# Mixer B's decode attention on the matrix engine, its K and V on GpSimd's queue

## The chip, the cores and the metric

One core of a Trainium2 chip runs one launch of the kernel. The metric is the device time of a launch in microseconds (us). The engines are PE (TensorE), DVE (VectorE), ACT (ScalarE) and POOL (GpSimd); SP issues most transfers. Each engine works through its own list of instructions in order and waits on semaphores for the others.

## What is computed

One layer of a hybrid decoder, at once for a prompt of 256 positions and for 8 decode samples of one position each (position 2048), 264 tokens in all:

- `h = RMSNorm(x)`, `z = h @ w_in`, cut into q, k, v of mixer A (16 heads, 2 kv heads) and of mixer B (16 heads of 64), with partial rotary on q and k.
- Mixer A: window of 128, with a learned sink for each head.
- Mixer B: keys at distances 0, d, 2d, ..., w for (w, d) = (128, 1), (512, 4), (2048, 16), merged by the branches' softmax denominators. For a decode sample these are 320 different keys of the cache and the sample's own, 321 in all; a key in several branches counts as often. With one softmax over the 321 keys, and log(count) added to the score, numerator and denominator are those of the merge:

```python
s = einsum('nqhd,nqjhd->nqhj', q, k[:, idx]) * 64 ** -0.5
p = exp(s - max(s)); l = sum(p); num = einsum('nqhj,nqjhd->nqhd', p, v[:, idx])
o_b = sum(exp(m - m_star) * num) / sum(exp(m - m_star) * l)      # over the three branches
```

- `x += RMSNorm(concat(RMSNorm(oA), RMSNorm(oB)) @ w_out)`, then a gated feed-forward part with a causal convolution of width 3.

## The kernel before

**Weights.** Everything is held transposed: 128 features on the partitions, 264 tokens along the row. Weights come in 364 chunks of 512 KB through a ring of four slots. For each chunk SP loads `raw`, ACT rounds it to `wh` (L499), DVE takes the rest as `wl` (L722), and PE does 24 matmuls, 8 tiles by 3 products: wh x hi, wh x lo, wl x hi (L1171 to L1173). SP loads chunk n once DVE has split chunk n-4; at step n ACT splits chunk n+3 and DVE chunk n+2, and then each does the stages of step n.

**The plan.** The first 84 steps (68 chunks of `w_in`, 16 of `w_out`) carry the attention between the chunks. `STEP` gives a step for each stage, `make_plan` writes `PLAN[n]`, and every engine goes through the same `PLAN[n]` after its part of chunk n. The three column groups of pair t (t = 0 to 3: four heads of mixer B, q, k and v) end at steps 12t+4, 12t+8 and e = 12t+12; they are taken out of PSUM by `evac` on DVE, which rotates q and k (L731 to L734). The prompt's heads follow as S (scores, L1234 and L1235), T (transposes of the probabilities, L1243) and V (values, L1260 to L1262), four heads in each pair.

**Mixer B, decode.** A unit u = 2t+v is two heads of all 8 samples; there are eight. Its stages before:

- `qk` (step e-3): PE transposes q and k of the 8 samples (L1209), ACT copies them (L529) and stores q to DRAM.
- `qI`: SP adds the samples' own key to `Kd` and loads q back, the same for all 128 partitions (`qb`, L434).
- `mul`: POOL multiplies `Kd`, keys on the partitions and 3 x 8 x 128 along the row, by `qb` (L1069). `bS`: DVE sums over the 64 features of each head (L872).
- `bT`: PE transposes the scores to 16 rows of 321 (L1297); DVE adds the mask and takes the minimum (L879), ACT does the exponentials (L571), DVE scales by 1/sum (L884).
- `pO`, `pI`: ACT stores the probabilities, SP loads them back spread over 2 x 64 partitions (`Pb`, L444).
- `bM`: POOL copies the own value in (L1076) and multiplies `Pb` by `Vd` (L1078). `bV`: ACT sums over the keys, 8 instructions (L582).

`Kd`, `Vd`, `qb`, `Pb` have one buffer each. SP loads K and V of the next unit (L450, L451, L457) in its own line with the weights, six steps ahead of the stage, after waiting for the reader of the buffer.

**Shared PSUM bank.** Of eight banks four take the projections, three the prompt's heads, and one, `B_M`, all the rest, in the order of the list `MISC`. PE waits in `take_misc` until the stage before has been copied out:

```python
n = misc(kind, *a)
if n:
    pe.wait_ge(misc_free, n)
```

V of the prompt is transposed in `vtr` (L1219) and copied by ACT (L518). Behind mixer B follow its norms (`N`, `W`, `ND`, from step 59 on), mixer A's heads (steps 57 to 74) and mixer A's decode attention, which is done by matmuls: `aload` (K and V, L1082, on POOL's queue, after the last sum of mixer B), `aS` (16 matmuls, L1269) and `aV` (16 matmuls, L1289).

Of the kernel before, what the change touches and what calls it, by code (L numbers as in the profile page):

```python
# [27 lines left out]
P = 128  # L28
# [8 lines left out]
NEG = 1e30  # L37
# [13 lines left out]
AHEAD = 6  # L51
# [46 lines left out]
def group_end(gi):  # L98
# [34 lines left out]
def make_plan():  # L133
# [8 lines left out]
    for t in range(4):  # L142
# [3 lines left out]
        add(e + STEP["qk"][0], "qk", t)  # L146
        add(e + 1, "vtr", t)
        for a in range(4):
            s0 = e + STEP["s"][t] + gap * a
            add(s0, "S", t, a)  # L150
            add(s0 + STEP["T"][t], "T", t, a)
            add(s0 + STEP["V"][t], "V", t, a)
        add(s0 + STEP["V"][t], "O", t)
        for v in range(2):
            add(e + STEP["qI"][v], "qI", 2 * t + v)
            add(e + STEP["mul"][v], "mul", 2 * t + v)
            add(e + STEP["bS"][v], "bS", 2 * t + v)
            add(e + STEP["bT"][v], "bT", 2 * t + v)
            add(e + STEP["pO"][v], "pO", 2 * t + v)
            add(e + STEP["pI"][v], "pI", 2 * t + v)  # L160
            add(e + STEP["bM"][v], "bM", 2 * t + v)
# [29 lines left out]
for _n in sorted(PLAN):  # L191
    for _s in PLAN[_n]:
# [3 lines left out]
        if s[0] in ("ss", "qk", "vtr", "vdec", "aS", "aT", "aR", "aV", "W", "ND", "bT")]  # L196
# [45 lines left out]
def build(nc, d, q_dram, p_dram):  # L242

    ctx = ExitStack()
    with ctx:
# [26 lines left out]
        with ExitStack() as att:  # L272
# [10 lines left out]
            qk = sa("qk", [NDEC, 512])  # L283
            vself = sa("vself", [P, 4, 2, NDEC])
# [13 lines left out]
            bSc = sa("bSc", [P, 48])  # L298
            bSm = sa("bSm", [16, KB])
            bP = sa("bP", [16, KB])  # L300
# [33 lines left out]
        bmn, bl, bri = (small[0:16, c:c + 1] for c in (78, 79, 80))  # L334
# [31 lines left out]
        Kd_landed, Kd_full, Vd_landed = sem("Kd_landed"), sem("Kd_full"), sem("Vd_landed")  # L366
        q_out, qb_landed, p_out, Pb_landed = sem("q_out"), sem("qb_landed"), sem("p_out"), sem("Pb_landed")
        kq_ready = sem("kq_ready")
        bS_ready, bV_ready = sem("bS_ready"), sem("bV_ready")
        vp_ready = sem("vp_ready")  # L370
# [7 lines left out]
        zero_ready = sem("zero_ready")  # L378
# [29 lines left out]
        def _(sp):  # L408
# [7 lines left out]
            def stage(kind, *a):  # L416
                if kind == "ss":

                    sp.wait_ge(misc_ready, misc("ss") + 1)
                    sp.wait_ge(zero_ready, 1)  # L420
                    load_K(0)
                    load_V(0)
                elif kind == "bS" and a[0] + 1 < OT:
                    load_K(a[0] + 1)
                elif kind == "bM" and a[0] + 1 < OT:
                    load_V(a[0] + 1)
                elif kind == "qI":

                    u, = a
                    t, v = u // 2, u % 2  # L430
                    sp.wait_ge(misc_free, misc("qk", t) + 1)
                    sp.dma_start(Kd[64:65, 2], qk[:, 256 + P * v:256 + P * v + P]).then_inc(Kd_full, 16)
                    sp.wait_ge(q_out, 16 * (t + 1))
                    sp.dma_start(qb[:], q_dram[t, :, P * v:P * v + P].unsqueeze(0).to_broadcast([P, NDEC, P])  # L434
                                 ).then_inc(qb_landed, 16)
                elif kind == "pI":

                    u, = a
                    sp.wait_ge(p_out, 16 * (u + 1))
                    if u:  # L440
                        sp.wait_ge(bV_ready, u)
# [1076 lines left out]
```

## Time and profile before

| what | value |
|---|---|
| three runs | 1321.42, 1323.63, 1326.42 us |
| median | 1323.63 us |
| span of the profiled execution | 1329.0 us |
| time around that span | none is given; the span is 5.4 us above the median |
| PE, DVE, ACT, POOL busy | 91, 60, 43, 17% of the span |
| mean granted PE clock | 0.951 of full speed (2.4 GHz) |
| moved by DMA | 236.99 MB |

The profile is of one execution. Times in its rows are us from the first instruction. Busy time of an engine is the union of its instructions' durations. PE's matmuls overlap each other in the records, so the pace of PE is read from start to start, not from durations. An fp32 matmul leaves two records, each with its weight load; one of fp32r, and a transpose, leave one. PEclk is the share of full speed that was granted: 1.00 is 2.4 GHz, 0.50 is 1.2 GHz, and a value between is a mean over a stretch that had both.

### The profile page before, as it was taken

What the parts mean: (1) busy time and instruction counts of PE and PEld (TensorE: products, weight loads), DVE (VectorE), ACT (ScalarE), POOL (GpSimd) and SP (SyncE); (2) the same over time, 40 slices, a digit from 0 to 9 for tenths busy, and PEclk for the clock granted to TensorE, in tenths of its full rate; (3) what the DMA queues carried; (4) which work ended last, traced back from release to release, by engine and by line L of the source; (5) the groups of instructions that cost most, each with busy time, mean ns of one, the idle gap of its engine ahead of it and who ended that gap; (6) DMA issues with size and microseconds to landing.
All of it is one profiled execution on the core that took longest, in us unless ns stands there. A gap on an engine that the chain in (4) does not pass through costs nothing.

```text
span 1329.0 us, 24539 instructions
## 1 busy us (share of the span) xinstructions
PE 1210.8 (91%) x9379; PEld 1182.2 (89%) x9379; DVE 791.0 (60%) x987; ACT 571.7 (43%) x938; POOL 223.3 (17%) x148
## 2 busy tenths in 40 slices
PE   5987687797989895999999999999999999999994
PEld 5987676786779895999999999999999999999994
DVE  5666969675644558665556655556655644454445
ACT  4334343446544364544444444444444433343331
POOL 2053525260200023410100100001010000020003
PEclk9998898897978997999999999999999999999997
DMA  6676969695522451455555555555555666656641
GB/s 250 230 236 219 294 196 282 202 260 147 140 80 80 140 166 58 146 188 173 189 187 174 173 167 189 184 189 167 169 185 174 205 187 176 183 178 179 184 143 65
DMA packets 83163, 236.99 MB, mean 178 GB/s; under 512 B 7432, under 2 KB 32368, under 8 KB 82032
## 3 DMA queue, kind: packets, MB, share of 16 engines
q1 hardware_dynamic: 81728, 232.30, 56.1%
q0 software_dynamic: 1072, 3.90, 0.9%
q8 instruction: 29, 0.48, 0.2%
q10 hardware_dynamic: 320, 0.20, 0.1%
q14 instruction: 14, 0.11, 0.0%
HBM read 231.13 MB, written 5.20 MB: 178 GB/s over the span
## 4 chain that ended last, share of the span: by engine, by line
PE 77%; DVE 10%; issue 5%; DMA 3%; ACT 2%; POOL 1%; SPq 0%; ACTq 0%; DVEq 0%; POOLq 0%
PE ps L1171 24%; PE ps L1172 24%; PE ps L1173 24%; DVE wl L722 2%; DMA raw<-in_w_in 2%; DVE bSc L872 1%; DVE bP L884 1%; PE ps L1235 1%; PE ps L1234 1%; DVE hl L957 1%; DVE xT L967 1%; DMA qb<-q_dram 1%; POOL Kd L1069 1%; PE ps L1243 1%; PE ps L1200 1%
## 5 line engine op out<-in xcount | busy, mean ns | idle before, releaser
L1171 PE MATMUL ps<-hh,wh 128*128 128x264 f32 x2080 | 610.2, 293 | 33.8 <-DVE wl L722 23.4
L1173 PE MATMUL ps<-hh,wl 128*128 128x264 f32 x2080 | 602.0, 289 | 0.0
L722 DVE TENSOR_TENSOR wl<-raw,wh 128x1024 fp32r<-128x1024 f32 x364 | 465.0, 1295 | 199.4 <-ACT wh L499 199.3
L1172 PE MATMUL ps<-hl,wh 128*128 128x264 f32 x1952 | 566.9, 290 | 0.0
L499 ACT CAST wh<-raw 128x1024 fp32r<-128x1024 f32 x364 | 374.9, 1045 | 352.1 <-PE ps L1173 276.6
L1171 PEld LDWEIGHTS ps<-hh,wh 128*128 128x128 f32 x2080 | 404.0, 194 | 44.8 <-DVE wl L722 27.2
L1173 PEld LDWEIGHTS ps<-hh,wl 128*128 128x128 f32 x2080 | 402.1, 193 | 0.0
L1172 PEld LDWEIGHTS ps<-hl,wh 128*128 128x128 f32 x1952 | 378.6, 194 | 0.1
L1172 PE MATMUL ps<-gl,wh 128*128 (+1 forms) x704 | 200.7, 285 | 0.0
L1171 PE MATMUL ps<-gh,wh 128*128 (+1 forms) x704 | 200.1, 284 | 0.0
L1173 PE MATMUL ps<-gh,wl 128*128 (+1 forms) x704 | 199.8, 284 | 0.0
L1172 PEld LDWEIGHTS ps<-gl,wh 128*128 128x128 f32 x704 | 132.7, 188 | 0.0
L1173 PEld LDWEIGHTS ps<-gh,wl 128*128 128x128 f32 x704 | 132.6, 188 | 0.0
L1171 PEld LDWEIGHTS ps<-gh,wh 128*128 128x128 f32 x704 | 132.5, 188 | 0.0
L1136 POOL COPY co<-U 128x4 f32 (+1 forms) x22 | 21.2, 963 | 395.7 <-DVE U L984 395.7
L1069 POOL TENSOR_TENSOR Kd<-Kd,qb 128x3072 f32<-128x3072 f32 x8 | 55.1, 6892 | 62.1 <-DMA qb<-q_dram 62.1
L983 DVE TENSOR_TENSOR U<-ps,rB 128x512 f32<-128x512 f32 x22 | 15.2, 692 | 75.2 <-PE ps L1173 75.1
L1078 POOL TENSOR_TENSOR Pb<-Pb,Vd 128x2568 f32<-128x2568 f32 x8 | 45.7, 5707 | 76.6 <-DMA Pb<-p_dram 76.6
L1003 DVE TENSOR_TENSOR up<-ps,rB 128x528 f32<-128x528 f32 x22 | 15.6, 707 | 69.5 <-PE ps L1173 69.5
L677 ACT ACTIVATE cv<-U,par 128x280 f32<-128x280 f32 x44 | 25.0, 616 | 64.3 <-DVE U L984 64.3
L1152 POOL TENSOR_TENSOR up<-up,ysq 128x528 f32<-128x528 f32 x5 | 9.6, 1918 | 243.2 <-ACT ysq L709 242.7
L991 DVE SCALAR_TENSOR_TENSOR cv<-U,par,cv 128x280 f32<-128x280 f32 x88 | 41.0, 507 | 11.4 <-ACT cv L677 8.3
(213 smaller groups left out, 1087.6 us busy)
## 6 DMA issues: line engine op xcount, KB each, us to landing
raw<-in_w_gate SPq DMA_DIRECT2D x88, 512.0 KB, 4.0
raw<-in_w_up SPq DMA_DIRECT2D x88, 512.0 KB, 4.6
raw<-in_w_down SPq DMA_DIRECT2D x88, 512.0 KB, 3.6
raw<-in_w_in SPq DMA_DIRECT2D x68, 512.0 KB, 6.6
raw<-in_w_out SPq DMA_DIRECT2D x32, 512.0 KB, 3.8
Pb<-p_dram SPq DMA_DIRECT2D x16, 642.0 KB, 8.8
Vd<-in_vb SPq DMA_DIRECT2D x8, 1280.0 KB, 8.4
Kd<-in_kb SPq DMA_DIRECT2D x8, 1024.0 KB, 5.7
```

The lines of the kernel that those rows point to most:

```text
L499: nc.scalar.copy(wh[:, slot], raw[:, slot]).then_inc(hi_ready, 1)
L677: nc.scalar.activation(cv[:, k], U[:, k, 0:NU - 2], ACT.Identity, scale=par[:, bass.ds(i * 2 + (C_CW + k), 1)], bias=par[:, bass.ds(i * 2 ...
L722: V.tensor_tensor(wl[:, slot], raw[:, slot], wh[:, slot].bitcast(F32), ALU.subtract).then_inc(lo_ready, 1)
L983: line.do(V.tensor_tensor(U[:, :, 2:2 + SEQ], ps[:, 0:2, 0:SEQ], wide(rB[:, 0:SEQ]), ALU.mult))
L991: ins = V.scalar_tensor_tensor(cv[:, k], U[:, k, tap:tap + NU - 2], par[:, bass.ds(i * 2 + (C_CW + FT * tap + k), 1)], cv[:, k], ALU.mult, ...
L1003: V.tensor_tensor(up[:], ps[:, 2:4, 0:TOK], wide(rB[:]), ALU.mult).then_inc(up_taken, 1)
L1069: G.tensor_tensor(Kd[:], Kd[:], qb[:].unsqueeze(1).to_broadcast([P, 3, NDEC, P]), ALU.mult).then_inc(kq_ready, 1)
L1078: G.tensor_tensor(Pb[:], Pb[:], Vd[:], ALU.mult).then_inc(vp_ready, 1)
L1136: line.do(G.tensor_copy(co[:, bass.ds(i * 2, 2), 0:2], U[:, :, SEQ:SEQ + 2]))
L1171: nc.tensor.matmul(out, a, x, start=start, stop=False)
L1172: nc.tensor.matmul(out, a, xl, start=False, stop=False)
L1173: return nc.tensor.matmul(out, b, x, start=False, stop=stop)
```

## The change

Mixer B's decode scores and values are computed by matmuls, with K held features-first and V keys-first (the arrays `kb` and `vb` swap their layouts on the host).

- Gone: `qk`, `qI`, `mul`, `bT`, `pO`, `pI`, `bM`, the two DRAM buffers, the buffers `Kd`, `qb`, `Vd`, `Pb`, and all of SP's stages (SP now loads only weights here). DVE's copy `vself` and its memset of `Kd` go too.
- `qsel` (POOL, step e-3, both units): the own key is copied into `Kt`, then q of the samples into `Qsel`, a zeroed array with 32 columns for each sample of which two are filled (one head each).
- `bS` (PE, steps e-2 and e+3): eight fp32 matmuls, 32 weight columns by 321 moving ones; sample 4q+j goes to PSUM partitions 32j to 32j+31, and q = 0 and 1 add up there. DVE's mask and ACT's exponential follow as before, on 128 partitions in place of 16. POOL then loads K for two units later; `Kt` has two buffers.
- `bR` (e, e+5): PE transposes the probabilities (three), ACT copies them to `pT`.
- `bV` (e+3, e+8): 24 fp32 matmuls, three blocks of keys for each of 8 samples, 128x128 weights from `Vk`, two moving columns; ACT copies out the two heads. POOL then loads V of the next unit into the one buffer `Vk`.
- `vdx` (e+1, right behind `vtr`): PE transposes v of the samples (two), ACT copies them to `v8`, POOL's queue brings them into row 64 of `Vk`'s last block.

```diff
@@ -104,17 +103,13 @@
-    "qI": [-3, 2],
-    "mul": [-2, 4],
-    "bS": [2, 6],
-    "bT": [3, 11],
-    "pO": [3, 11],
-    "pI": [3, 12],
-    "bM": [7, 15],
-    "bV": [8, 16],
+    "qsel": [-3, -3],
+    "vdx": [1],
+    "bS": [-2, 3],
+    "bR": [0, 5],
+    "bV": [3, 8],
-    "qk": [-3],
...
@@ -152,13 +147,9 @@
-            add(e + STEP["qI"][v], "qI", 2 * t + v)
-            add(e + STEP["mul"][v], "mul", 2 * t + v)
+            add(e + STEP["qsel"][v], "qsel", 2 * t + v)
-            add(e + STEP["bT"][v], "bT", 2 * t + v)
-            add(e + STEP["pO"][v], "pO", 2 * t + v)
-            add(e + STEP["pI"][v], "pI", 2 * t + v)
-            add(e + STEP["bM"][v], "bM", 2 * t + v)
+            add(e + STEP["bR"][v], "bR", 2 * t + v)
...
@@ -193,7 +184,7 @@
         ORDER.setdefault(_s[0], []).append(_s[1:])
 MISC = [s for n in sorted(PLAN) for s in PLAN[n]
-        if s[0] in ("ss", "qk", "vtr", "vdec", "aS", "aT", "aR", "aV", "W", "ND", "bT")]
+        if s[0] in ("ss", "vtr", "vdx", "vdec", "aS", "aT", "aR", "aV", "W", "ND", "bS", "bR", "bV")]
 def number(kind, *args):
...
@@ -307,10 +298,8 @@
-                Kd = sb("Kd", [P, 3, NDEC, P], F32, a2)
-                qb = sb("qb", [P, NDEC, P], F32, a2)
-                Vd = sb("Vd", [P, NDEC, KB], F32, a2)
-                Pb = sb("Pb", [P, NDEC, KB], F32, a2)
+                Kt = sb("Kt", [P, 2, NDEC, KB], F32, a2)
+                Vk = sb("Vk", [P, 3, NDEC, P], F32, a2)
...
@@ -519,17 +460,12 @@
+                elif kind == "vdx":
+                        act.wait_ge(Vk_full, 16 * 2 * t)
+                    nc.scalar.copy(v8[:], ps[0:NDEC, B_M, 0:256]).then_inc(misc_free, 1)
...
@@ -565,24 +501,26 @@
+                elif kind == "bS":
+                    if u:
+                        act.wait_ge(misc_ready, misc("bR", u - 1) + 1)
+                elif kind == "bR":
+                    act.wait_ge(misc_ready, misc(kind, *a) + 1)
+                    line.do(nc.scalar.copy(pT[:, 0:256], ps[:, B_M, 0:256]))
+                    nc.scalar.copy(pT[0:65, 256:384], ps[0:65, B_M, 256:384]).then_inc(misc_free, 1)
+                elif kind == "bV":
+                    act.wait_ge(misc_ready, misc(kind, *a) + 1)
+                    for h in range(2):
+                        ins = nc.scalar.copy(od[64 * h:64 * h + 64, 0, u], ps[64 * h:64 * h + 64, B_M, h:h + 15:2])
+                        if h == 0:
+                    ins.then_inc(misc_free, 1)
...
@@ -864,20 +799,12 @@
-                    u, = a
-                    dve.wait_ge(kq_ready, u + 1)
-                    if u:
-                        dve.wait_ge(misc_ready, misc("bT", u - 1) + 1)
-                    V.tensor_reduce(bSc[:], Kd[:].rearrange("p c s (h e) -> p (c s h) e", h=2), AX.X,
-                                    ALU.add).then_inc(bS_ready, 1)
-                elif kind == "bT":
-                        dve.wait_ge(p_out, 16 * u)
+                        dve.wait_ge(b_exp, u)
-                        out=bSm[:], in0=ps[0:16, B_M, 0:KB], in1=tab[0:16, T_MD:T_MD + KB], scale=1.0, scalar=NEG,
+                        out=bSm[:], in0=ps[:, B_M, 0:KB], in1=tab[:, T_MD:T_MD + KB], scale=1.0, scalar=NEG,
...
@@ -1060,25 +987,50 @@
+                elif kind == "ss":
+                    pool.wait_ge(misc_ready, misc(kind) + 1)
+                    load_K(0)
+                    load_V(0)
+                    load_K(1)
+                elif kind == "qsel":
+                    t, v = u // 2, u % 2
+                    pool.wait_ge(Kt_landed[v], 16 * (t + 1))
+                    pool.wait_ge(evac_done, GI[("kB", t)] + 1)
+                    if u:
+                        pool.wait_ge(qsel_ready, 3 * u)
+                    G.tensor_copy(Kt[:, v, :, KEYS_B], ks[:, t % 2, v, SEQ:TOK]).then_inc(qsel_ready, 1)
+                    place = Qsel[:, v].rearrange("p (q r) -> p q r", q=2)
+                    q2 = qs[:, t % 2, v, SEQ:TOK].rearrange("p (q j) -> p q j", q=2)
+                    for h in range(2):
+                        pool.wait_ge(qsel_ready, 3 * u + 1 + h)
+                        G.tensor_copy(place[64 * h:64 * h + 64, :, h:h + 97:32],
+                                      q2[64 * h:64 * h + 64]).then_inc(qsel_ready, 1)
+                elif kind == "bS":
+                    if u + 2 < OT:
+                        pool.wait_ge(misc_ready, misc(kind, *a) + 1)
+                        load_K(u + 2)
+                elif kind == "vdx":
+                    t, = a
+                    pool.wait_ge(misc_free, misc(kind, *a) + 1)
+                    load_vself(2 * t)
+                elif kind == "bV":
+                    u, = a
+                    if u + 1 < OT:
+                        pool.wait_ge(misc_ready, misc(kind, *a) + 1)
+                        load_V(u + 1)
+                        if u % 2 == 0:
+                            load_vself(u + 1)
+                    pool.wait_ge(misc_ready, misc("bV", OT - 1) + 1)
...
@@ -1088,6 +1040,18 @@
+            def load_K(u):
+                G.dma_start(Kt[:, u % 2], d["kb"][u]).then_inc(Kt_landed[u % 2], 16)
+            def load_V(u):
+                G.dma_start(Vk[:, 0:2], d["vb"][u, :, 0:2]).then_inc(Vk_landed, 16)
+                G.dma_start(Vk[0:64, 2], d["vb"][u, 0:64, 2]).then_inc(Vk_landed, 16)
+            def load_vself(u):
+                v = u % 2
+                G.dma_start(Vk[64:65, 2], v8[:, P * v:P * v + P]).then_inc(Vk_full, 16)
+            G.memset(Qsel[:], 0.0)
...
@@ -1199,15 +1163,12 @@
+                elif kind == "vdx":
+                    pe.wait_ge(evac_done, GI[("vB", t)] + 1)
+                    for m in range(2):
+                        ins = nc.tensor.transpose(ps[0:NDEC, B_M, P * m:P * m + P], vT[:, m, SEQ:TOK], ident[:])
...
@@ -1290,12 +1251,34 @@
-                elif kind == "bT":
-                    pe.wait_ge(bS_ready, a[0] + 1)
+                elif kind == "bS":
+                    u, = a
+                    pe.wait_ge(qsel_ready, 3 * (u + 1))
+                    take_misc(kind, *a)
+                    v = u % 2
+                    for q in range(2):
+                        for j in range(4):
+                            ins = nc.tensor.matmul(ps[32 * j:32 * j + 32, B_M, 0:KB],
+                                                   Qsel[:, v, P * q + 32 * j:P * q + 32 * j + 32],
+                                                   Kt[:, v, 4 * q + j], start=q == 0, stop=q == 1)
+                    ins.then_inc(misc_ready, 1)
+                elif kind == "bR":
+                    u, = a
+                    pe.wait_ge(b_p, u + 1)
-                        ins = nc.tensor.transpose(ps[0:16, B_M, k0:k1], bSc[0:k1 - k0, 16 * c:16 * c + 16],
-                                                  ident[0:k1 - k0, 0:k1 - k0])
+                        ins = nc.tensor.transpose(ps[0:k1 - k0, B_M, P * c:P * c + P], bP[:, k0:k1], ident[:])
+                    ins.then_inc(misc_ready, 1)
+                elif kind == "bV":
+                    u, = a
+                    pe.wait_ge(Vk_landed, 32 * (u + 1))
+                    pe.wait_ge(Vk_full, 16 * (u + 1))
+                    take_misc(kind, *a)
+                    for s in range(NDEC):
+                        r = 32 * (s % 4) + 2 * (s // 4)
+                        for c, (k0, k1) in enumerate(KSPLIT_B):
+                            ins = nc.tensor.matmul(ps[:, B_M, 2 * s:2 * s + 2], Vk[0:k1 - k0, c, s],
+                                                   pT[0:k1 - k0, P * c + r:P * c + r + 2], start=c == 0, stop=c == 2)
```

## Rows read from the trace of the kernel before

**Rows 1.** The page: the span, and PE's busy time.

```profile
span 1329.0 us, 24539 instructions
PE 1210.8 (91%) x9379; PEld 1182.2 (89%) x9379; DVE 791.0 (60%) x987; ACT 571.7 (43%) x938; POOL 223.3 (17%) x148
```

**Rows 2.** Windows: busy us (x instructions) by engine, PEclk, DMA share, GB/s; then L722's own.

```profile
47.80:316.10 268.30, 216.10 (x1541) 202.06 (x1540) 200.49 (x237) 115.10 (x282) 105.53 (x33) 0.90 0.79 239
590.00:690.00 100.00, 100.00 (x819) 100.00 (x818) 60.25 (x76) 44.08 (x56) 10.05 (x15) 1.00 0.56 177
...
47.80:316.10 268.30, 87.09 (x53) 0.90 0.79 239
316.10:459.00 142.90, 29.20 (x24) 0.87 0.36 102
590.00:690.00 100.00, 39.74 (x34) 1.00 0.56 177
```

**Rows 3.** Groups by line and shape, 0 to 520 us: busy us, mean ns, idle before.

```profile
L722 DVE TENSOR_TENSOR wl<-raw,wh 128x1024 fp32r<-128x1024 f32 x102 | 146.4, 1444 | 37.8 <-ACT wh L499 37.7
L1069 POOL TENSOR_TENSOR Kd<-Kd,qb 128x3072 f32<-128x3072 f32 x8 | 55.1, 6892 | 62.1 <-DMA qb<-q_dram 62.1
L884 DVE TENSOR_SCALAR bP<-bP,small 16x321 f32<-16x321 f32 x8 | 29.5, 3691 | 0.3
L582 ACT ACTIVATE Pb<-Pb 128x321 f32<-128x321 f32 x64 | 29.1, 457 | 1.8 <-POOL Pb L1078 1.8
L872 DVE TENSOR_REDUCE bSc<-Kd 128x48 f32<-128x3072 f32 x8 | 26.8, 3344 | 6.7 <-POOL Kd L1069 6.7
L518 ACT COPY vn<-ps 128x512 f32<-128x512 f32 x4 | 2.3, 586 | 3.9 <-PE ps L1219 3.9
```

**Rows 4.** Timeline of POOL, then of DVE, 138 to 155 us: start us, us, instruction.

```profile
138.74 5.69 POOL L1078 TENSOR_TENSOR Pb<-Pb,Vd 128x2568 f32<-128x2568 f32 x1 [9.59 <-DMA Pb<-p_dram]
147.34 6.99 POOL L1069 TENSOR_TENSOR Kd<-Kd,qb 128x3072 f32<-128x3072 f32 x1 [2.91 <-DMA qb<-q_dram]
...
139.45 5.16 DVE L884 TENSOR_SCALAR bP<-bP,small 16x321 f32<-16x321 f32 x1
147.81 7.08 DVE L734 TENSOR_TENSOR qs<-r,sh 128x528 f32<-128x528 f32 x1
```

**Rows 5.** Timeline of PE, 69 to 71 us and 76 to 78 us.

```profile
69.14 0.60 PE L1219 MATMUL ps<-ident,vT 128*128 128x128 f32 x4
69.67 0.49 PE L1234 MATMUL ps<-ks,qs 64*128 64x128 f32 x2
69.99 0.59 PE L1235 MATMUL ps<-ks,qs 64*128 64x256 f32 x2
70.52 0.39 PE L1171 MATMUL ps<-hh,wh 128*128 128x264 f32 x1
...
76.78 0.33 PE L1260 MATMUL ps<-vn,PT 128*128 128x64 f32 x2
77.47 0.45 PE L1297 MATMUL ps<-ident,bSc 128*16 128x128 f32 x3
```

**Rows 6.** Windows around mixer A's decode matmuls, columns as in rows 2.

```profile
392.60:394.30 1.70, 1.70 (x27) 1.62 (x27) 1.54 (x5) 0.74 (x3) 0.00 (x0) 0.99 0.07 22
394.30:401.10 6.80, 6.80 (x37) 6.76 (x35) 1.39 (x5) 1.61 (x5) 0.00 (x0) 0.50 0.27 77
418.60:421.50 2.90, 2.90 (x21) 2.66 (x19) 0.00 (x0) 2.48 (x6) 0.00 (x0) 1.00 0.00 1
421.50:425.30 3.80, 3.80 (x16) 3.53 (x15) 0.00 (x0) 3.41 (x8) 0.00 (x0) 0.51 0.00 0
425.30:428.40 3.10, 3.10 (x15) 3.10 (x15) 2.86 (x8) 0.00 (x0) 0.00 (x0) 0.50 0.00 0
```

**Rows 7.** Waits of SP's queue, 47.8 to 316.1 us; POOL's timeline at 354 us.

```profile
SPq L450 <- DVE bSc L872: 33.3, 7, 8.2
...
354.01 0.59 POOL L1082 DMA_DIRECT2D KtA<-in_ka  x1 [12.16 <-ACT Pb L582]
```

More of the change, by code:

```diff
@@ L145, in make_plan @@
         gap = STEP["gap"][t]
-        add(e + STEP["qk"][0], "qk", t)
         add(e + 1, "vtr", t)
+        add(e + STEP["vdx"][0], "vdx", t)
         for a in range(4):
@@ L297, in build @@
             rd = sa("rd", [P, 3, NDEC])
[L298 to L300 removed]
+            bSm = sa("bSm", [P, KB])
+            bP = sa("bP", [P, KB])
             with ExitStack() as a2:
@@ L333, in build @@
         amn, al, aes, ari = (small[:, c:c + 1] for c in (74, 75, 76, 77))
-        bmn, bl, bri = (small[0:16, c:c + 1] for c in (78, 79, 80))
+        bmn, bl, bri = (small[:, c:c + 1] for c in (78, 79, 80))
         sinkn = small[:, 82:82 + H_A + 1]
@@ L365, in build @@
         KtA_landed, VtA_landed, VtA_full = sem("KtA_landed"), sem("VtA_landed"), sem("VtA_full")
[L366 to L370, printed above, removed]
+        Kt_landed = [sem(f"Kt_landed{c}") for c in range(2)]
+        Vk_landed, Vk_full = sem("Vk_landed"), sem("Vk_full")
+        qsel_ready = sem("qsel_ready")
         norm_a = sem("norm_a")
@@ L414, in load @@
                 sp.dma_start(raw[:, slot], src).then_inc(raw_landed[slot], 16)
[L416 to L427, printed above, removed]
-                    u, = a
[L430 to L439, printed above, removed]
-                    if u:
-                        sp.wait_ge(bV_ready, u)
-                    for h in range(2):
-                        src = p_dram[u].rearrange("(s h) k -> h s k", h=2)[h].unsqueeze(0)
-                        sp.dma_start(Pb[64 * h:64 * h + 64], src.to_broadcast([64, NDEC, KB])).then_inc(Pb_landed, 16)
-            def load_K(u):
-                if u:
-                    sp.wait_ge(bS_ready, u)
-                sp.dma_start(Kd[:, 0:2], d["kb"][u, :, 0:2]).then_inc(Kd_landed, 16)
-                sp.dma_start(Kd[0:64, 2], d["kb"][u, 0:64, 2]).then_inc(Kd_landed, 16)
-            def load_V(u):
-                if u:
-                    sp.wait_ge(vp_ready, u)
-                sp.dma_start(Vd[:, :, 0:KEYS_B], d["vb"][u]).then_inc(Vd_landed, 16)
             sp.dma_start(par[:, 0:C_CW], d["par"][:, 0:C_CW]).then_inc(gains_landed, 16)
@@ L469, in _ @@
                 load(chunk(n, 0, 4, 0), d["w_in"][GROUPS[n // 4][2], n % 4])
-                for s in PLAN.get(n - AHEAD, ()):
-                    stage(*s)
             with sp.Fori(0, (N_OUTA + N_OUTB) // 4) as i:
@@ L747, in evac @@
                     dve.wait_ge(v_stored, 16 * 4)
-                    dve.wait_ge(misc_ready, misc("vtr", 3) + 1)
+                    dve.wait_ge(misc_ready, misc("vdx", 3) + 1)
                     line.do(V.tensor_tensor(vT[:, 0], src[:, 1], rB[:], ALU.mult))
@@ L780, in evac @@
                         dve.wait_ge(v_stored, 16 * t)
-                        dve.wait_ge(misc_ready, misc("vtr", t - 1) + 1)
-                    line.step(V.tensor_tensor(vT[:], src, wide(rB[:]), ALU.mult))
-                    V.tensor_copy(vself[:, t], vT[:, :, SEQ:TOK]).then_inc(evac_done, 1)
+                        dve.wait_ge(misc_ready, misc("vdx", t - 1) + 1)
+                    V.tensor_tensor(vT[:], src, wide(rB[:]), ALU.mult).then_inc(evac_done, 1)
             def stage(kind, *a):
@@ L798, in stage @@
                     line.step(V.memset(qA[:], 0.0))
-                    V.memset(Kd[64:128, 2], 0.0).then_inc(zero_ready, 1)
                 elif kind == "S":
```

63 lines of the change are left out of this document (12 added, 51 removed).

## The prediction

> **What bounds the kernel now.** I read the page first: PE is busy 1210.8 of 1329.0 us [rows 1], so the question is where the rest of PE's time is and whether mixer B's decode work owns it. The splits of L722, one for each weight chunk, give the pace: 34 in 100 us from 590 to 690, so 2.94 us a chunk when nothing but weights is multiplied, with PE at 100 of 100 us and a granted clock of 1.00 [rows 2]. The change touches nothing after the projections, so that stage stays as it is. From 47.8 to 316.1, where mixer B's prompt and decode attention run, 53 splits take 268.3 us, PE is busy 216.1 and the clock is 0.90 [rows 2].
>
> I take those 268.3 us apart. Chunks: 53 x 2.94 = 155.8. A prompt head costs PE 0.85 for its scores (69.67 to 70.52), about 0.40 for three transposes and 0.69 for its values (76.78 to 77.47) [rows 5]; 16 heads x 1.94 = 31.0. The transposes of V take 0.53 (69.14 to 69.67) [rows 5], four times 2.1; the transposes "qk" are as many and as large, 2.0; those of the scores ("bT") three each time, 0.40 x 8 = 3.2. That makes 194 us of work. PE is idle for 268.3 - 216.1 = 52. The remaining 22 is what the half clock costs (a clock of 0.90 is 54 us at 1.2 instead of 2.4 GHz, worth at most 27). So 74 us of the stage are not PE work, and 194 are.
>
> Why PE idles is in the DVE and POOL rows. While POOL multiplies Pb (138.74, 5.69 us), DVE's 16x321 scaling of bP lasts 5.16; while it multiplies Kd (147.34, 6.99 us), DVE's last step of a rotation lasts 7.08 [rows 4]. Over all, L884 took a mean of 3.7 us and L722 1.44 us, against 1.17 in the clean stretch (39.74 / 34) [rows 2, 3]. PE's next chunk needs DVE's split, so it stands. DVE's sums over Kd (8 x 3.3) add to it. That is what the change removes.
>
> **The change, part by part.**
>
> *POOL's products, DVE's sums, ACT's sums.* Gone: 55.1 us for Kd on POOL and the product of Pb, 26.8 on DVE, 29.1 and more on ACT [rows 3], none of it PE's. What they are worth is the idle time they cause. I take 49 of the 52 us of idle and all 22 of the old half clock, since the drops follow idle stretches. Bounds: 40 and 52 of the first, 12 and 22 of the second.
>
> *Transposes qk and bT*: 2.0 + 3.2 = 5.2 us less on PE.
>
> *Scores by matmul (bS).* Eight fp32 matmuls a unit, 32 weight columns, 321 moving. An upper end from the scores: L1234 with 128 columns starts 0.32 before L1235, which with 256 takes 0.53 [rows 5], so 0.21 for 128 columns and 0.53 for 321: 4.2 us a unit, 34 in eight. A lower end: if only the issue of the narrow weights counted, 16 records at the pace of L1269's 65-column weights (27 records in 1.70 us, 0.063 each [rows 6]) are 1.0 us, 8 in eight. The upper row shares passes and length, the lower the narrow weights, and neither the four places in PSUM; I take the middle, 2.6, so 21 us.
>
> *Values by matmul (bV).* 24 fp32 matmuls a unit, 128x128 weights, two moving columns. The nearest row is the prompt's values, 128x128 weights and 64 columns: three in 0.69, 0.23 each [rows 5]. So 5.5 us a unit, 44 in eight. The moving side cannot make it shorter than the weights' load, and L1289 took 6.8 us for 16 of them, part of it at half clock (418.6 to 425.3) [rows 6], so 44 is near its lower end and 55 the upper one.
>
> *What bV does to the clock.* Both stretches of small decode matmuls lost it. During L1269, with 16 columns, the clock went from 0.99 to 0.50 and stayed there from 394.3 to 401.1; L1289 began at 418.6 at 1.00, was at 0.51 from 421.5 and the projections behind it at 0.50 until 428.4 [rows 6]. PE was never idle in these rows: 6.8 us at half clock, 3.4 us of work lost, each time. bV moves fewer columns and lasts longer, so I charge 3.4 to each: 27 us. Bounds: 14 if every second unit escapes, 40 if the matmuls of bS behind it stay in the slow stretch.
>
> *Transposes bR and vdx*: 8 x 0.4 + 4 x 0.3 = 4.4 us.
>
> *New waits.* All of these share one PSUM bank, and each waits until the one before is copied out. vdx stands directly behind vtr, whose copy takes ACT 0.59 (L518 [rows 3]); bS of the odd unit stands directly behind bV of the even one. With the way there and back I take 0.9 us each, eight times: 7. Bounds 4 and 12. Queued behind them on PE is the next chunk. Behind DVE's and ACT's waits for bS is the next split, but both are two chunks ahead (5.9 us), and their part of bS is some 2 us, so that costs nothing; without that lead it would be 2 us a unit.
>
> *Copies.* ACT's copies of pT and od replace 64 sums; DVE's masks cover 128 partitions in place of 16 with the same 321 columns. Nothing, hidden behind PE.
>
> *Loads.* K and V move to POOL's queue in place of SP's. SP no longer stands at waits before its weight loads (33.3 us at L450 alone [rows 7]), and qb and Pb (128 x 1024 and 128 x 2568 floats, 0.5 + 1.3 MB a unit) are no longer written; the stage ran at 239 GB/s with a DMA share of 0.79 [rows 2], and 8 x 1.8 MB over 268 us take 54 GB/s off. POOL's order is stores, three small copies (qsel), K, V: V has five steps, over 20 us, from its issue to its use. K and V are cut into fewer, longer rows. Cost nothing; bounds 0 and 10 (first case below).
>
> *Outside the stage.* The last sums of ACT ended only when POOL's load of KtA was released, at 354.0 us [rows 7], among mixer A's heads, whose exponentials wait behind them; from 316.1 to 459.0 24 splits took 142.9 us [rows 2]. I take 8 us gained, bounds 3 and 12. The memset of Kd at the start is 0.9 us less.
>
> **Sum.** Added: 21 + 44 + 27 + 4.4 + 7 = 104. Removed: 49 + 22 + 5.2 + 8 + 0.9 = 85. Net +19 us. The profiled execution's span of 1329.0 us is 5.4 above the median of the runs, 1323.6 (1321.4 to 1326.4), and no time around the span is shown; a difference of parts carries over to the median: 1343.
>
> **Rivals.**
>
> *Slower still: weight loads come late.* K and V now run beside the weight loads and share the DMA engines with them, where before they stood in one line. For it: the stage's share is 0.79 already. Against: fewer bytes. With 10 us of it and bS at 4.2 (+13) the sum is +42, 1366. Chance 0.15. The Trainium skill's page DMA: Bandwidth & Descriptors, section Issuing engines are not separate DMA queues, says that transfers interleave on the same 16 engines whichever engine issues them; by that a queue of their own gains K and V nothing. The traces so far neither show nor refute it.
>
> *Column groups overlap.* The four outputs of bS lie in four groups of 32 partitions; if the matmuls ran beside each other, bS would be 1.0 us in place of 2.6: -13, so 1330. For it, the order of the matmuls alternates the groups; against it, no row shows two matmuls at once. Chance 0.20, within 0.5% or just slower. The Trainium skill's page TensorE: Matmul & The Clock Gate, Part 3: Packing small matmuls, says that matmuls in different column groups run concurrently; by it bS is near a quarter of its serial time.
>
> *Faster: the clock holds through bV.* Its place is the eight bV and the chunk behind each; its price 27 us. Then the sum is 19 - 27 = -8, 1315. It decides from six of the eight on (19 / 3.4 = 5.6). For it: bV stands among dense chunks, and PE is never idle. Against: L1269 and L1289 stood so too, and both lost it. Chance 0.20; with overlapping columns as well, 1302.
>
> **How the numbers follow.** The forecast's own case has 0.45, its own range 1332 to 1355. A difference of 0.5% (6.6 us) is about what a measurement of this kernel can tell from none. Slower by more than that: 0.45 + 0.15 minus a little for good bounds of idle, plus half of the overlap case, 0.62. Within: 0.15, from the overlap case and the edge of the forecast. Faster: 0.23, the clock case and a part of the overlap case in which the removed idle was worth more. The range for 8 in 10 is 1310 to 1366: the clock case and the slow case lie within or at its ends.
>
> **What would show it.** Right: from 48 to 316 us PE's idle falls from 52 to under 10 us, no DVE instruction lasts over 2 us, L722 is back at 1.2; the 24 matmuls of bV take 5.5 us or more; half-clock stretches begin inside bV and run on into the chunk behind. bS at 4 us shows the serial price, at 1 to 2 the overlap. Wrong: a clock of 1.00 behind bV, bV under 5 us, PE idle over 25 us because raw weights or V land late, or qsel on POOL coming after PE is ready for bS.

## The result, and the profile after

The changed kernel takes 1341.54 us (median of 4 runs, 1337.18 to 1343.58) against 1323.35 before (4 runs, 1321.42 to 1326.42): a ratio of 1.0132, 95% interval 1.0101 to 1.0162. It is slower, by 18 us; the forecast was 1343.0. Which steps of the forecast were right, and which only cancelled, is the matter of what follows.

The profiled execution took 1342.7 us. The page of the changed kernel, the part that answers to [rows 1]:

```profile
span 1340.9 us, 25396 instructions
PE 1269.3 (95%) x9883; PEld 1234.4 (92%) x9883; DVE 700.7 (52%) x974; ACT 549.1 (41%) x842; POOL 143.9 (11%) x181
```

PE is busy 58.5 us more while the span is 11.9 us longer: PE waits less and works more. DVE lost 90 us of work, POOL 79 and ACT 23.

Windows of the changed kernel (busy us of PE, PEld, DVE, ACT, POOL, then PEclk, DMA share, GB/s), cut where PE starts the same weight chunks in both kernels: chunk 7, chunk 59, chunk 83. Behind the two stages is a clean stretch, and then the surroundings of one bV:

```profile
44.10:335.60 291.50, 282.22 (x2033) 262.10 (x2032) 111.88 (x221) 93.95 (x197) 30.69 (x66) 0.87 0.53 174
335.60:469.00 133.40, 121.11 (x880) 110.76 (x879) 71.45 (x175) 67.97 (x157) 0.00 (x0) 0.94 0.31 96
590.00:690.00 100.00, 100.00 (x819) 100.00 (x818) 59.61 (x73) 44.18 (x55) 8.69 (x12) 1.00 0.53 174
...
78.20:80.60 2.40, 2.40 (x24) 2.40 (x23) 0.00 (x0) 0.00 (x0) 0.00 (x0) 1.00 0.10 39
80.60:90.80 10.20, 9.68 (x51) 7.97 (x51) 0.69 (x4) 1.23 (x5) 2.15 (x4) 0.50 0.26 88
90.80:94.00 3.20, 3.20 (x24) 2.72 (x24) 3.17 (x6) 0.68 (x1) 0.00 (x0) 1.00 1.02 347
```

The same two stages in the kernel before, cut by the same chunks:

```profile
44.80:310.90 266.10, 213.91 (x1526) 200.43 (x1525) 197.85 (x231) 112.52 (x275) 105.53 (x33) 0.90 0.80 243
310.90:456.10 145.20, 129.44 (x882) 118.69 (x881) 74.86 (x179) 72.01 (x175) 7.49 (x5) 0.87 0.37 104
```

The stage of mixer B grew from 266.1 to 291.5 us (+25.4) although PE's time outside its instructions fell from 52.2 to 9.3 us. The stage behind it shrank from 145.2 to 133.4 (-11.8): its clock rose from 0.87 to 0.94. Half clock costs at most (1 - clock) of a stretch (less where PE is idle in it), so at most 18.9 us there became at most 8.0. From chunk 107 on both take 752.7 us. Above all the last three lines of the first fence: bV starts at a clock of 1.00, PE never stops inside it, and 2.4 us on the clock is at 0.50 for 10.2 us.

The timeline of PE in the changed kernel at the first scores and at the first values, answering to [rows 5] (start us, us, instruction, records):

```profile
58.40 1.29 PE L1261 MATMUL ps<-Kt,Qsel 128*32 128x321 f32 x16 [2.20 <-POOL Qsel L1010]
59.61 0.39 PE L1135 MATMUL ps<-hh,wh 128*128 128x264 f32 x1
...
78.22 8.19 PE L1280 MATMUL ps<-pT,Vk 128*128 128x2 f32 x48
86.92 2.37 PE L1261 MATMUL ps<-Kt,Qsel 128*32 128x321 f32 x16 [0.53 <-ACT od L520]
89.22 0.59 PE L1135 MATMUL ps<-hh,wh 128*128 128x264 f32 x1
```

L1261 is bS, 1.22 us from start to start at full clock and 2.30 at half. L1280 is bV: 8.71 us here, 60.7 in all eight units. Groups of the changed kernel up to 520 us, answering to [rows 3, 4] (busy us, mean ns, idle before):

```profile
L660 DVE TENSOR_TENSOR wl<-raw,wh 128x1024 fp32r<-128x1024 f32 x102 | 123.7, 1221 | 52.8 <-ACT wh L440 52.6
L811 DVE TENSOR_SCALAR bP<-bP,small 128x321 f32<-128x321 f32 x8 | 3.1, 390 | 0.3
L672 DVE TENSOR_TENSOR qs<-r,sh 128x528 f32<-128x528 f32 x8 | 5.7, 707 | 0.3
L520 ACT COPY od<-ps 64x8 f32<-64x8 f32 x16 | 2.5, 159 | 53.5 <-PE ps L1280 53.3
L1171 PE MATMUL ps<-ident,vT 128*8 128x128 f32 x8 | 1.5, 270 | 3.1 <-ACT vn L459 3.1
```

The scaling of bP now covers 128 partitions and takes 0.39 us; on 16 partitions it had taken 3.69. The last step of a rotation is 0.71 us where one had taken 7.08 [rows 3, 4]. SP's queue, in [rows 7] at L450 for 33.3 us, now waits for one thing only (44 to 336 us; us, times, longest):

```profile
SPq L400 <- DVE wl L660: 271.9, 52, 16.6
```

### The profile page after: what moved, and what is told of

It is laid out like the page before. It is cut to its first block, busy times and chain, and to the rows that moved or that the text cites. A ratio compares the mean times of both kernels' runs of the same rounds, so it can differ in the third digit from the quotient of the medians.

```text
span 1340.9 us, 25396 instructions
## 1 busy us (share of the span) xinstructions
PE 1269.3 (95%) x9883; PEld 1234.4 (92%) x9883; DVE 700.7 (52%) x974; ACT 549.1 (41%) x842; POOL 143.9 (11%) x181
## 4 chain that ended last, share of the span: by engine, by line
PE 90%; DVE 4%; issue 2%; ACT 1%; POOL 0%; DVEq 0%; ACTq 0%; POOLq 0%
PE ps L1135 26%; PE ps L1136 26%; PE ps L1137 26%; PE ps L1280 4%; PE ps L1261 1%; PE ps L1196 1%; PE ps L1195 1%; PE ps L1204 1%; DVE hl L884 1%; DVE xT L894 1%; PE ps L1164 1%; PE ps L1222 1%; PE ps L1223 1%; DVE yT L965 0%; DVE yT L966 0%
## 5 line engine op out<-in xcount | busy, mean ns | idle before, releaser
L660 DVE TENSOR_TENSOR wl<-raw,wh 128x1024 fp32r<-128x1024 f32 x364 | 442.3, 1233 | 213.4 <-ACT wh L440 213.2
L1280 PEld LDWEIGHTS ps<-pT,Vk 128*128 128x128 f32 (+1 forms) x384 | 59.0, 247 | 1.0 <-issue 1.0
L1280 PE MATMUL ps<-pT,Vk 128*128 128x2 f32 (+1 forms) x384 | 59.2, 290 | 0.0
L475 ACT ACTIVATE Sm<-Sm,small 128x128 f32<-128x128 f32 x32 | 12.9, 403 | 77.6 <-DVE small L751 77.6
```

What stands on the lines that cost most here:

```text
L660: V.tensor_tensor(wl[:, slot], raw[:, slot], wh[:, slot].bitcast(F32), ALU.subtract).then_inc(lo_ready, 1)
L1280: ins = nc.tensor.matmul(ps[:, B_M, 2 * s:2 * s + 2], Vk[0:k1 - k0, c, s], pT[0:k1 - k0, P * c + r:P * c + r + 2], start=c == 0, stop=c == 2)
```

## The theories

**A.** bV is too expensive, mostly by what it does to the clock: narrow moving sides on full 128x128 weights take PE down to 1.2 GHz, for themselves and for the chunks behind. **B** (rival): the clock falls for another reason, and the price is the load of 24 weights, narrow or not. Two more questions: do the four places of bS in PSUM run beside each other, whatever the order; and what had PE's idle time been before, POOL's products or the transfers that served them?

## Experiments

**e1: bV moves 64 columns in place of 2.** The columns around the wanted two are multiplied too, and four copies pick the right ones.

```diff
...
-                        r = 32 * (s % 4) + 2 * (s // 4)
+                        r = 64 * (s % 4 // 2)
...
-                            ins = nc.tensor.matmul(ps[:, B_M, 2 * s:2 * s + 2], Vk[0:k1 - k0, c, s],
-                                                   pT[0:k1 - k0, P * c + r:P * c + r + 2], start=c == 0, stop=c == 2)
+                            ins = nc.tensor.matmul(ps[:, B_M, 64 * s:64 * s + 64], Vk[0:k1 - k0, c, s],
+                                                   pT[0:k1 - k0, P * c + r:P * c + r + 64], start=c == 0, stop=c == 2)
```

> Edit against the changed kernel: the 24 matmuls of bV move 64 columns of the probabilities in place of 2 (the 62 others are computed and dropped), and ACT picks its columns with four copies in place of two. The weights, their count and their order are the same, and the weights' loads (0.11 us a record) still set the pace, since the prompt's values with 64 columns take 0.23 us a matmul. Theory A, the clock falls because bV's matmuls move almost nothing: it holds now, the half-clock stretches of 10.2 us behind seven of the eight bV go or shrink to 3.4, L1280 falls from 59 to some 45 us in all, and the time from 1341.5 to 1295 to 1315 us although PE computes more. Theory B, the clock falls for the weight loads or for what stands around bV: no change of the clock, time 1341 to 1350. Theory C, the waits on the shared PSUM bank are the cost: no change, or 1 to 2 us more for the two further copies.

Measured 1312.98 us, ratio to before 0.9902 (0.9867 to 0.9937). 32 times the arithmetic in bV makes the kernel about 29 us faster than the change itself, and faster than the kernel before. Windows of this kernel, the stage and then the second bV:

```profile
44.10:306.30 262.20, 252.26 (x2033) 233.58 (x2032) 112.03 (x223) 94.85 (x213) 31.04 (x66) 0.98 0.59 193
...
104.50:109.80 5.30, 5.30 (x51) 5.30 (x49) 2.39 (x3) 0.48 (x1) 0.55 (x1) 1.00 0.64 228
```

The weights are the same 24, and bV costs 5.3 to 6.2 us a unit, 45.9 in all. Three stretches at half clock are left in the stage, of 3.4 us each, two of them behind a bV. Theory A holds for the clock, and B falls there: the same loads at the same pace do not take it down. What the loads cost at full clock stays (e6). The stage is 29.3 us shorter than in the changed kernel, and its half clock costs 0.02 x 262 = 5 us against 0.13 x 291.5 = 38.

**e2: bV spread between the chunk's own matmuls,** three of its matmuls behind every three of the chunk's.

```diff
...
                        ins = mm3(ps[:, bank + m, 0:TOK], (slot, 256 * k + P * m), xh[:, kt0 + k], xl[:, kt0 + k],
                                  first and k == 0, last and k == 3)
+                        if between is not None:
+                            between(2 * k + m)
...
```

> Edit against the changed kernel: the 24 matmuls of bV, the same ones, are issued three at a time between the 24 of the chunk of their own step, in place of all behind it. Theory A, the clock falls in a stretch of several us in which only small matmuls run: now the dense ones are spread among them, the half-clock stretches go, bV costs its 5.4 us a unit, and the time is 1295 to 1315 us. If the small ones lower the clock even at a third of the time, 1330 to 1345. Theory C, waits on the shared bank: unchanged but for the copy of bV, that now has the rest of the step to hide in: 1335 to 1341.

Measured 1357.33 us, ratio 1.0251 (1.0212 to 1.029). Outside all three ranges: worse than the change, not better. Timeline and windows of this kernel:

```profile
79.42 0.72 PE L1284 MATMUL ps<-pT,Vk 128*128 128x2 f32 x6
80.00 0.37 PE L1135 MATMUL ps<-hh,wh 128*128 128x264 f32 x1
...
82.97 1.27 PE L1284 MATMUL ps<-pT,Vk 128*128 128x2 f32 x6
```

```profile
78.40:82.00 3.60, 3.60 (x35) 3.60 (x33) 0.00 (x0) 0.00 (x0) 0.00 (x0) 1.00 0.37 137
82.00:92.20 10.20, 10.20 (x53) 8.38 (x54) 1.51 (x5) 1.91 (x5) 2.15 (x4) 0.50 0.44 138
...
44.10:349.30 305.20, 293.51 (x2032) 270.95 (x2031) 111.92 (x221) 93.18 (x197) 30.87 (x66) 0.83 0.51 166
```

The narrow matmuls last the same (six records 0.58 us from start to start), but now the clock is at half for 13.7 us in six of the eight units, and more of the chunk's matmuls lie in it. By the clock that is up to 0.17 x 305 = 52 us lost in the stage against 38, which accounts for the 13.7 us by which the stage is longer. Dense neighbours between the narrow matmuls do not save the clock. Why it gets worse rather than stays equal is not settled; that the narrow matmuls now reach over a longer stretch is only an argument.

**e3: the order of bS,** places outside and halves inside, so that two neighbours always share a place.

```diff
-                    for q in range(2):
-                        for j in range(4):
+                    for j in range(4):
+                        for q in range(2):
```

> Edit against the changed kernel: the eight matmuls of bS in the order of the column group first (both samples of group 0, then of group 1, ...), in place of the groups in turn. In the changed kernel 16 records of bS take 1.22 us at the full clock, though one alone moves 321 columns, 0.27 us by the scores' 256 columns: the groups must run beside each other. If it is the turn-taking that lets them, the records now take 2.2 to 4.4 us a unit, and the time rises by 8 to 25 us, to 1350 to 1366. If the order does not matter, 1341.

Measured 1335.41 us (1332.29 to 1344.76, 7 runs), ratio 1.0072 (1.0042 to 1.0101), which touches the interval of the change at 1.0101. That is under both expected times: no cost for the other order, and whether the 0.6% between the two ratios is a gain is not settled. In the trace, which is of the longest of the seven runs, bS takes 1.24 us at full clock where it took 1.22. In either order four records start within 0.02 (changed kernel) and 0.04 us (here) of each other (58.395, 58.402, 58.409, 58.415 in the changed kernel; 58.514, 58.527, 58.544, 58.558 here) and the next four 0.29 us behind the first. So matmuls run at once, whichever order they are issued in. The records do not name their place in PSUM. That the four are of four different places, so that PE takes some ahead of others of the list, is inferred, not shown.

**e4: K and V on SP's queue again,** issued there six steps behind the stage that frees their buffer. Nothing else moves.

```diff
...
+                elif kind == "bV" and a[0] + 1 < OT:
+                    sp.wait_ge(misc_ready, misc(kind, *a) + 1)
+                    load_V(a[0] + 1)
...
             for n in range(4, N_IN):
                 load(chunk(n, 0, 4, 0), d["w_in"][GROUPS[n // 4][2], n % 4])
+                for s in PLAN.get(n - 6, ()):
+                    stage(*s)
```

> Edit against the changed kernel: K and V are issued by SP between its weight loads again, six steps behind them, with the same waits for the matmuls that free the buffers; the samples' own v stays on POOL's queue. My account leaves the queue out: the weight loads have room in both, so 1339 to 1345, and PE's idle time stays at 12 to 15 us. If the queue of its own is worth something, weight loads stand behind 1.3 MB of K or V and SP's waits, and it is slower by 5 to 15 us; if POOL's queue costs something (K and V late, DVE or PE waiting), faster by as much.

Measured 1341.05 us, ratio 1.0121 (1.0085 to 1.0157): the queue alone is worth nothing that these runs can tell. Waits of SP's queue in this kernel, 44 to 336 us (us, times, longest):

```profile
SPq L400 <- DVE wl L682: 170.1, 50, 10.5
SPq L415 <- PE ps L1282: 71.2, 7, 12.0
SPq L412 <- PE ps L1263: 23.9, 6, 8.3
```

SP stands 95 us in waits ahead of weight loads, and PE waits no more than before: the four slots cover it. The Trainium skill's page DMA: Bandwidth & Descriptors, section Issuing engines are not separate DMA queues, says that the issuing engine matters only for the time of the issue; this run agrees, with 1341.05 against 1341.54.

**b1: the kernel before with POOL's products on one sample.** It leaves out the products of the other seven; all transfers and waits stay.

```diff
-                    G.tensor_tensor(Kd[:], Kd[:], qb[:].unsqueeze(1).to_broadcast([P, 3, NDEC, P]),
-                                    ALU.mult).then_inc(kq_ready, 1)
+                    G.tensor_tensor(Kd[:, 0, 0], Kd[:, 0, 0], qb[:, 0], ALU.mult).then_inc(kq_ready, 1)
...
-                    G.tensor_tensor(Pb[:], Pb[:], Vd[:], ALU.mult).then_inc(vp_ready, 1)
+                    G.tensor_tensor(Pb[:, 0], Pb[:, 0], Vd[:, 0], ALU.mult).then_inc(vp_ready, 1)
```

> Edit against the kernel before: POOL's two products take one sample of eight each (128x128 and 128x321 elements in place of 128x3072 and 128x2568); the products of the other seven are left out. Transfers, DVE's and ACT's sums, transposes and every wait stay. It measures the side that the change removed. Theory A, DVE's instructions stand while POOL multiplies and PE stands behind DVE: the 5 to 7 us durations on DVE go, PE's idle time over the first 60 chunks falls from 54 to 10 to 25 us, the half-clock stretches there mostly go, and the time is 1265 to 1290 us. If the round trips through DRAM (Pb, qb) or SP's waits were the real cost and the products only lay beside them, 1305 to 1325.

Measured 1296.23 us, ratio 0.9766 (0.9738 to 0.9794), between the two ranges. So the products cost some 29 us of the kernel before. One group of this kernel says through what; it is the scaling on DVE that had taken 3.69 us [rows 3]:

```profile
L884 DVE TENSOR_SCALAR bP<-bP,small 16x321 f32<-16x321 f32 x8 | 3.4, 426 | 0.3
```

Only POOL's work changed, and it takes 0.43: the slow DVE instructions came from POOL's products. But PE still stands for 40 us of the stage. Where, the next run shows.

**b2: b1 with qb and Pb loaded for one sample too.** It leaves out those loads of the other seven samples, and ACT sums the same sample eight times. SP's order, its waits and the round trips through DRAM stay.

```diff
...
-                        src = p_dram[u].rearrange("(s h) k -> h s k", h=2)[h].unsqueeze(0)
-                        sp.dma_start(Pb[64 * h:64 * h + 64], src.to_broadcast([64, NDEC, KB])).then_inc(Pb_landed, 16)
+                        src = p_dram[u].rearrange("(s h) k -> h s k", h=2)[h, 0:1].unsqueeze(0)
+                        sp.dma_start(Pb[64 * h:64 * h + 64, 0:1], src.to_broadcast([64, 1, KB])).then_inc(Pb_landed, 16)
...
```

> The kernel before with the POOL products on one sample of eight, as in b1, and with qb and Pb loaded for that one sample too (64 KB and about 80 KB a load in place of 512 and 642 KB); it leaves out the products and the loads of the other seven samples. In b1 the products were gone and 40 us of PE's idle time stayed in the stage. If what is left is the volume of the transfers (the raw w_in tiles wait behind the broadcast reads), the idle time falls under 25 us, the waits of ACT for raw w_in fall with it, and the time is 1265 to 1285 us. If it is the order of SP's issues and their waits for POOL and for the round trips through DRAM, the idle time stays near 40 us and the time at 1290 to 1300 us.

Measured 1264.59 us, ratio 0.9547 (0.9514 to 0.9579), 0.4 us under the range expected for the volume. Windows of b1 and of b2, the stage of 52 chunks in each, then the waits of PE and ACT in it; b1:

```profile
44.60:287.60 243.00, 203.51 (x1526) 191.60 (x1525) 137.46 (x229) 112.53 (x275) 22.73 (x33) 0.93 0.91 266
...
PE ps L1242 <- ACT Sm L541: 32.3, 5, 11.6
PE ps L1259 <- ACT PT L549: 3.3, 2, 2.8
...
ACT wh L499 <- DMA raw<-in_w_in: 76.6, 21, 12.8
```

and b2:

```profile
44.40:252.70 208.30, 197.93 (x1525) 186.48 (x1524) 136.43 (x229) 113.14 (x275) 20.16 (x33) 0.98 0.77 254
...
PE ps L1242 <- ACT Sm L541: 3.0, 3, 1.4
...
ACT wh L499 <- DMA raw<-in_w_in: 31.4, 15, 8.9
```

In b1 the DMA share is 0.91. PE does not stand at a chunk but at a head, where the transposes wait for ACT's probabilities; ACT is held in its own list at the split of a weight chunk that has not landed. With the volume of qb and Pb gone the wait falls from 32.3 to 3.0 us and the clock is 0.98. SP still stands 82 us of the stage in waits for other things than DVE's splits, against 100 in b1, so those waits by themselves did not hold PE; one of them, for POOL at L457, fell from 33.8 to 1.1 us, and a part of it in the gain is not excluded. The kernel before shows the same two waits of PE; the third line is ACT's:

```profile
PE ps L1243 <- ACT Sm L541: 29.8, 7, 8.7
PE ps L1260 <- ACT PT L549: 12.1, 5, 3.9
...
ACT wh L499 <- DVE bP L884: 33.9, 7, 6.8
```

In before ACT's split stood 33.9 us behind DVE's slow scaling of bP, and 3.1 in b1: so the products reached PE through ACT's list. Between before and b1 PE's second wait falls to 3.3 and the first stays; between b1 and b2 the first goes. The stage falls by 23 us with the products and by 35 more with the loads. Of PE's idle time (starts more than 0.6 us apart, less 0.2 each) 53.9 became 40.4 and then 11.2. Taken away in this order, the loads owned more than the products; the loads alone were not tried.

**e5: bV with one block of keys of three.** It leaves out the values of 256 of the 321 keys and keeps the block with 65 rows of weights; loads, transposes and waits stay.

```diff
-                        for c, (k0, k1) in enumerate(KSPLIT_B):
-                            ins = nc.tensor.matmul(ps[:, B_M, 2 * s:2 * s + 2], Vk[0:k1 - k0, c, s],
-                                                   pT[0:k1 - k0, P * c + r:P * c + r + 2], start=c == 0, stop=c == 2)
+                        ins = nc.tensor.matmul(ps[:, B_M, 2 * s:2 * s + 2], Vk[0:65, 2, s],
+                                               pT[0:65, 2 * P + r:2 * P + r + 2], start=True, stop=True)
```

> Edit against the changed kernel: bV does one of its three key blocks, 8 matmuls in place of 24 a unit; the values of the other 256 keys are left out. Theory A: L1280's line falls from 60.7 us in all to 15 to 20, the half-clock stretches of 10.2 us behind bV go or fall to 3.4, and the time is 1270 to 1290 us, a gain well over the 29 us that 128 matmuls take at the full clock. If the clock does not follow bV, the gain is 29 to 35 us only: 1306 to 1312.

Measured 1287.73 us, ratio 0.9712 (0.9685 to 0.9738). A third of the matmuls is 44.0 us less in bV (60.7 to 16.7), of which some 29 are pace at full clock, and the whole gain is about 54: the rest is clock. The clock of this stage is 0.97:

```profile
44.30:277.40 233.10, 224.36 (x1776) 208.07 (x1776) 112.17 (x223) 93.97 (x197) 31.44 (x66) 0.97 0.66 217
```

Eight narrow matmuls in a row are followed by a drop of 3.4 us in three of the eight units and by none in the others; 24 cost 10.2 in six of eight.

**e6: the sides of bV exchanged.** The probabilities become the weights (32 columns, as in bS), V is what moves (128 columns), and four samples go to four places of PSUM. The result comes out transposed, so a step later two transposes bring it back.

```diff
...
+                    for q in range(2):
+                        for c, (k0, k1) in enumerate(KSPLIT_B):
+                            for j in range(4):
+                                ins = nc.tensor.matmul(ps[32 * j:32 * j + 32, B_M, P * q:P * q + P],
+                                                       pT[0:k1 - k0, P * c + 32 * j:P * c + 32 * j + 32],
+                                                       Vk[0:k1 - k0, c, 4 * q + j], start=c == 0, stop=c == 2)
+                    ins.then_inc(misc_ready, 1)
+                elif kind == "bO":
+                    take_misc(kind, *a)
+                    for q in range(2):
+                        ins = nc.tensor.transpose(ps[:, B_M, P * q:P * q + P], o8[:, P * q:P * q + P], ident[:])
...
```

> Edit against the changed kernel: in bV the operands change places. The probabilities are the weights (32 columns, one column group for each of four samples) and V moves (128 columns); ACT copies the result (128x256) to SBUF, and a step later PE turns it back with two transposes and ACT picks the heads. Four groups run beside each other, as the records of bS show (four start within 0.02 us). 24 matmuls are six rounds of two records of 0.11 us: 1.3 to 1.6 us a unit in place of 7.6, and 0.4 for the transposes; the moving side is busy, so the clock holds: 1270 to 1290 us, faster than both kernels. If 32 weight columns do not hold the clock, or the extra turn through the shared bank costs more than 1 us a unit: 1290 to 1305.

Measured 1281.88 us (1281.23 to 1283.4, 5 runs), ratio 0.9676 (0.9659 to 0.9693): faster than both kernels, 43 us below before in the same comparison. Against the changed kernel that is 0.9676 / 1.0132 = 0.955, worked out from the two ratios. Timeline and windows of this kernel:

```profile
78.13 1.52 PE L1289 MATMUL ps<-Vk,pT 128*32 128x128 f32 x48
80.23 1.29 PE L1270 MATMUL ps<-Kt,Qsel 128*32 128x321 f32 x16 [0.58 <-ACT o L522]
```

```profile
44.30:272.10 227.80, 218.08 (x2049) 199.17 (x2048) 112.04 (x223) 96.27 (x205) 30.57 (x66) 1.00 0.69 222
```

The same 24 matmuls take 1.45 us from start to start in place of 7.6 on the mean, 14.3 in all eight units with the waits behind four of them, and the clock is 1.00 through the stage.

## Why the prediction came out right, and where it did not

The working was made against the profiled execution, and there the change is +11.9 us (1329.0 to 1340.9), not the forecast +19. The profiled execution of before was a long one: with the 1.8 us that the run of after has around its span (1342.7 against 1340.9) it took an estimated 1330.8, 7.4 over its median, and that of after is 1.2 over its own. The two medians differ by 18.2. So the hit on the median owes some 6 us to that: "a difference of parts carries over to the median" did not hold to better than this. That the median lies within 2 us of the forecast is luck; the direction is not.

| term | forecast, us | measured, us |
|---|---|---|
| idle time of PE, with the new waits | -49 + 7 = -42 | 53.9 to 12.1: -41.8 |
| old half clock of the stage | -22 | 27.3, less 7.6 that lay over idle time: -19.7 |
| qk and bT | -5.2 | 1.4 + 2.0: -3.4 |
| outside the stage, with the memset | -8.9 | -0.7 ahead, -11.8 and -0.9 behind: -13.4 |
| bS | +21 | 8 x 1.22: +9.8 |
| bV at full clock | +44 | 43.2, less 2.1 of waits already in the first row: +41 |
| clock behind bV | +27 | 39.3, less 2.3 over idle time: +37 |
| bR, vdx | +4.4 | 2.4 + 0.9: +3.3 |

The measured terms add to +13 us, the spans say +11.9. Half clock that lies over idle time costs nothing: in the stage of before PE was idle in 15 of the 54.6 us at half clock, in that of after in 4.6 of 78.5. For bV, time at half clock is counted half. That agrees with the records at full clock: 24 of them in the 2.40 us from 78.2, 16 in 1.7 to 1.8 in e5, so 48 take 4.8 to 5.4 us.

**Right.** Idle time, bV's pace (the row of the prompt's values carried over: 0.22 a matmul against 0.23), its place on the path, the half clock that begins inside bV and runs on into the next chunk, no cost in the loads and their queue. The waits on the shared bank are small: 3.1 us for vdx behind vtr (L1171) and 2.1 for bS behind bV, where they were put, and once 1.8 for vtr (L1180) behind the copy of bR; 7.0 in all against 7. No group of DVE in the stage has a mean over 1.22 us. The rival of late weight loads did not come: the stage's DMA share fell from 0.80 to 0.53.

**Wrong: bS.** "The upper row shares passes and length, the lower the narrow weights, and neither the four places in PSUM; I take the middle, 2.6." It measured 1.22 at full clock, just over the lower end. The rival of overlapping column groups is what happened, though by itself it did not bring the time down to its 1330. The sentence "no row shows two matmuls at once" was true of the rows and a poor guide. The Trainium skill's page TensorE: Matmul & The Clock Gate, Part 3: Packing small matmuls, says that matmuls in different column groups run concurrently; the trace agrees, with eight matmuls of 321 columns in 1.22 us.

**Wrong: the size of the clock term.** "bV moves fewer columns and lasts longer, so I charge 3.4 to each." The direction was right, the size was not: behind six of the eight bV the stretch is 10.2 us long, 5.1 us lost, and behind the last two 6.8. A ninth stretch, of 3.4 us at 305.9, begins behind no bV but after a wait of PE of 1.8 us. The rows it was read from, 16 moving columns and 32 records, had 6.8 us at half clock [rows 6]; 48 records with 2 columns bring 10.2. This is within the given bounds (14 to 40), at their top, and nearly cancels the error in bS.

**Wrong: how PE came to idle.** "PE's next chunk needs DVE's split, so it stands." In the stage of before PE waited 3.2 us for L722 and 42 for ACT's probabilities of the prompt's heads. DVE's slow instructions did reach PE, but through ACT, whose split stood 33.9 us behind L884. b1 and b2 put some 13 us of idle time on POOL's products and 29 on the volume of qb and Pb, which the prediction had counted only as bandwidth set free. The size of the term came out right because the change removes both causes at once.

**Wrong: the gain behind the stage.** It was put down to ACT's sums and the late KtA. KtA was issued 12 us ahead of chunk 59, where it had been 43 behind, but the window's half clock can account for nearly all of the 11.8: at most 18.9 us down to 8.0. Why that clock rose was not tried, so an indirect part of KtA is not excluded. b1, where KtA comes 42 us behind chunk 59, already shows 139.8 us there in place of 145.2, at a clock of 0.90.

The rival "the clock holds through bV" did not come for this kernel, but e1 is its test. Where the clock holds the time is 1313. That is close to the 1315 forecast for this rival, but bS overlaps in e1 too, and for both together the forecast was 1302.

## What to carry to other kernels

A small fp32 matmul between dense ones was priced here by its weight load and by what it did to the clock for the microseconds behind it, not by its arithmetic: put the operand with few columns on the weight side, so that the long one moves and several lie beside each other in PSUM (7.6 us became 1.5 here). Idle time of an engine names a stage, not a cause: before pricing what a change removes, follow PE's wait to the engine in front and ask what that one's own list was held by. And a difference worked out from one profiled execution is no better than the distance of that execution from its median.

## What was not expected of the hardware

- More work made the kernel faster: 64 moving columns in place of 2 on the same 24 weights, 1341.5 to 1313.0 us, since the clock went from 0.87 to 0.98 in the stage.
- PE was busy inside bV while the clock fell (78.2 to 80.6 us: 2.40 of 2.40 busy, then 0.50).
- The same narrow matmuls, mixed evenly with dense ones, cost more clock (0.83) than in one block (0.87).
- Of the fp32 matmuls with 32 weight columns, whose results go to four places of PSUM, four records start within 0.02 to 0.04 us of each other, whichever order they are issued in.
- A DVE scaling of 16x321 floats took 3.69 us on the mean beside POOL's large products and 0.43 beside small ones, over eight times as long for an instruction that shares no buffer with them.
